# Transposing the SwiGLU activations on TensorE into PSUM instead of on VectorE in SBUF

## The reference

```
h = rms_norm(x); proj = h @ w_in                      # 1024 x 7428
merged = sum over 4 mixers of sigmoid(gate_n) * (mixer_n(proj) @ w_branch_n)
x = x + merged @ w_out                                # 1024 x 1024
h = rms_norm(x)
gate, up = split(h @ w_up)                            # 1024 x 2 * 2816
x = x + (silu(gate) * up) @ w_down                    # 2816 x 1024
```

## Time and profile before

| | before |
|---|---|
| median of 3 runs | 854.22 us |
| the profiled execution | 854.05 us |
| its span in the profile | 852.2 us |
| PE busy | 846.0 us (99%) |
| PE weight loads busy | 703.4 us (83%) |
| DVE busy | 665.1 us (78%) |
| ACT busy | 445.9 us (52%) |
| POOL busy | 114.8 us (13%) |
| DVE transposes (L1349), 192 instructions | 79.4 us |

### The profile page before, as it was taken

The page is one execution under the profiler, slowest core; times in us unless marked ns, Lnnn a source line. Parts: engine busy times, 40 slices in busy tenths (PEclk is TensorE's granted clock), DMA queues, the critical chain, the costliest instruction groups (busy, mean ns, idle before and its releaser), DMA issues.

```text
span 852.2 us, 11120 instructions
## 1 busy us (share of the span) xinstructions
PE 846.0 (99%) x4158; PEld 703.4 (83%) x4158; DVE 665.1 (78%) x1034; ACT 445.9 (52%) x646; POOL 114.8 (13%) x89
## 2 busy tenths in 40 slices
PE   9999999999999999999999999999999999999998
PEld 8888888888888888878888888888888888888787
DVE  7885967768778999985479668768697799999843
ACT  6557654754454444444365675558443644444441
POOL 0750201005502000000005402010054000000000
PEclk9999999999999999999999999999999999999999
DMA  9846655465567666556566365665655576666541
GB/s 341 289 156 188 201 181 173 145 227 194 177 196 241 197 195 192 191 187 192 154 188 185 112 194 163 198 198 146 221 186 169 168 225 196 198 197 194 178 148 49
DMA packets 87814, 160.46 MB, mean 188 GB/s; under 512 B 7504, under 2 KB 14160, under 8 KB 87760
## 3 DMA queue, kind: packets, MB, share of 16 engines
q1 hardware_dynamic: 87328, 159.09, 59.5%
q10 hardware_dynamic: 432, 0.66, 0.2%
HBM read 158.68 MB, written 1.05 MB: 187 GB/s over the span
## 4 chain that ended last, share of the span: by engine, by line
PE 96%; DVE 3%; issue 0%
PE bulk L1696 29%; PE bulk L1700 29%; PE bulk L1697 29%; PE bankAB L1444 2%; DVE wide L1349 2%; DVE w_lo L1024 1%; PE bulk L1752 1%; PE bankT L1601 0%; PE bankAB L1590 0%; PE bulk L1724 0%; PE bulk L1730 0%; PE bulk L1743 0%; PE bankAB L1548 0%; PE bankAB L1453 0%; DVE wide L1337 0%
## 5 line engine op out<-in xcount | busy, mean ns | idle before, releaser
L1024 DVE TENSOR_TENSOR w_lo<-raw,w_hi 128x1024 fp32r<-128x1024 f32 (+1 forms) x288 | 361.8, 1272 | 100.4 <-ACT w_hi L750 98.2
L750 ACT ACTIVATE w_hi<-raw 128x1024 fp32r<-128x1024 f32 (+1 forms) x286 | 296.6, 1047 | 244.9 <-PE bulk L1700 241.7
L1696 PE MATMUL bulk<-w_hi,hT_hi 128*128 128x512 f32 (+1 forms) x880 | 342.9, 390 | 0.0
L1697 PE MATMUL bulk<-w_lo,hT_hi 128*128 128x512 f32 (+1 forms) x880 | 339.2, 385 | 0.0
L1700 PE MATMUL bulk<-w_hi,hT_lo 128*128 128x512 f32 (+1 forms) x880 | 336.3, 386 | 0.0
L1696 PEld LDWEIGHTS bulk<-w_hi,hT_hi 128*128 128x128 f32 x880 | 165.3, 188 | 33.2 <-issue 0.5
L1700 PEld LDWEIGHTS bulk<-w_hi,hT_lo 128*128 128x128 f32 x880 | 165.0, 188 | 33.2
L1697 PEld LDWEIGHTS bulk<-w_lo,hT_hi 128*128 128x128 f32 x880 | 165.3, 188 | 31.8
L1349 DVE STREAM_TRANSPOSE wide<-wide 32x256 f32<-32x256 f32 (+1 forms) x192 | 79.4, 414 | 3.1
L1696 PE MATMUL bulk<-w_hi,aT_hi 128*128 128x512 f32 x174 | 68.0, 391 | 2.6 <-DVE wide L1337 2.6
L1700 PE MATMUL bulk<-w_hi,aT_lo 128*128 128x512 f32 x174 | 67.7, 389 | 0.0
(11 more groups left out here) (248 smaller groups left out, 708.9 us busy)
## 6 DMA issues: line engine op xcount, KB each, us to landing
raw<-in_w_in_dram SPq DMA_DIRECT2D x110, 512.0 KB, 4.2
raw<-in_w_ffn_up_dram SPq DMA_DIRECT2D x80, 512.0 KB, 3.8
raw<-in_w_ffn_down_dram SPq DMA_DIRECT2D x44, 512.0 KB, 3.4
raw<-in_w_branch_dram SPq DMA_DIRECT2D x20, 512.0 KB, 4.2
raw<-in_w_out_dram SPq DMA_DIRECT2D x16, 512.0 KB, 3.3
bias<-in_b_gate_dram SPq DMA_DIRECT2D x16, 256.0 KB, 4.7
raw<-in_w_ffn_up_dram SPq DMA_DIRECT2D x16, 256.0 KB, 3.5
raw<-in_w_in_dram SPq DMA_DIRECT2D x10, 256.0 KB, 2.6
```

The costliest lines, as they stand in the source:

```text
L750: act.activation(w_hi[:, g % RING, :, 0:width], raw[:, g % RAW, :, 0:width], ACT.Copy).then_inc(hi_ready, 1)
L1024: vec.tensor_tensor(w_lo[:, g % RING, :, 0:width], raw[:, g % RAW, :, 0:width], w_hi[:, g % RING, :, 0:width].bitcast(F32), ALU.subtract). ...
L1696: pe.matmul(dst, hi, whi, start=(k == ks[0]), stop=False)
L1697: pe.matmul(dst, hi, wlo, start=False, stop=False)
```

## The change

`act_turn` and its event go away. PE gets a stage `tr_act` p: for each token tile it waits for `ff_ready`, takes a bank (A and B for even p, T and O for odd p), and transposes the four blocks of 128 columns (two in the last part) into it. It stands at PE's slot FIRST(`ffu` p) + 6, for the last part at LAST(`fflast`) + 3. `act_evac` waits for that stage, reads the PSUM bank instead of `wide`, and stands at the same slot (before: three slots later; for the last part at LAST + 9). `ff_up` waits from p = 2 on until PE has read the buffer it overwrites.

```diff
+for _p in range(NPAIR):
+    _PE += [(FIRST[("ffu", _p)] + 6, "tr_act", _p)]
+_PE += [(LAST["fflast"] + 3, "tr_act", NPAIR)]
...
-FF_DONE = [FIRST[("ffu", _p)] + 4 for _p in range(NPAIR)] + [LAST["fflast"] + 1]
-FF_TURN = [_u + 1 for _u in FF_DONE[:-1]] + [FF_DONE[-1] + 4]
...
-        ffn += [(FIRST[("ffu", p)], "ff_gate", p)]
-    ffn += [(FF_DONE[NPAIR], "ff_gate", NPAIR)]
-    for p, u in enumerate(FF_DONE):
-        ffn += [(u, "ff_up", p), (FF_TURN[p] + 4, "act_evac", p)]
-        ffn += [(FF_TURN[p] + a, "act_turn", p, a) for a in range(NQUAD)]
+        ffn += [(FIRST[("ffu", p)], "ff_gate", p), (FIRST[("ffu", p)] + 4, "ff_up", p), (FIRST[("ffu", p)] + 6, "act_evac", p)]
+    ffn += [(LAST["fflast"] + 1, "ff_gate", NPAIR), (LAST["fflast"] + 1, "ff_up", NPAIR),
+            (LAST["fflast"] + 3, "act_evac", NPAIR),
...
             def act_evac(layer, p):                       # ACT
-                act.wait_ge(act_turned, nth(act_turned, layer, p))
-                for t in range(TT):
-                    lhs_part(layer, ("act", p, t), act_columns(aT[0], p, t), turned_act(p)[:, t, :, :])
+                blocks = 4 if p < NPAIR else 2
+                for t in range(TT):
+                    act.wait_ge(stage_done, nth(stage_done, layer, ("tr_act", p, t)))
+                    lhs_part(layer, ("act", p, t), aT[0][:, 4 * p:4 * p + blocks, t * P:(t + 1) * P],
+                             bank[("AB", "TO")[p % 2][t]][:, 0:blocks * P].rearrange("p (k q) -> p k q", k=blocks))
...
                     vec.wait_ge(ff_gated, nth(ff_gated, layer, (p, t)))
+                    if p >= 2:
+                        vec.wait_ge(stage_done, nth(stage_done, layer, ("tr_act", p - 2, t)))
...
-            def act_turn(layer, p, a):
-                if a == 0:
-                    vec.wait_ge(ff_ready, nth(ff_ready, layer, (p, 1)))
-                blocks, at = FF_BLOCKS[p], 2560 + 1024 * (p % 2)
-                tokens = slice(a * QUAD, (a + 1) * QUAD)
-                source = wide[tokens, :, at:at + blocks * P].rearrange("p t (k b q) -> p t k b q", b=NQUAD, q=QUAD)
-                for b in range(NQUAD):
-                    last = vec.transpose(turned_act(p)[b * QUAD:(b + 1) * QUAD, :, :, tokens], source[:, :, :, b, :])
-                if a == NQUAD - 1:
-                    last.then_inc(act_turned, 1)
...
+            def tr_act(layer, p):                         # PE
+                blocks = 4 if p < NPAIR else 2
+                for t in range(TT):
+                    pe.wait_ge(ff_ready, nth(ff_ready, layer, (p, t)))
+                    name = ("AB", "TO")[p % 2][t]
+                    take(name, lhs_lo, layer, ("act", p, t))
+                    for k in range(blocks):
+                        ins = pe.transpose(bank[name][:, k * P:(k + 1) * P], ff_act(t, p, blocks * P)[:, k * P:(k + 1) * P], identity)
+                    ins.then_inc(stage_done, 1)
```

More of the change, by code:

```diff
@@ L181, in stage_parts @@
         return [((stage, args[0], t), ("AB", "TO")[args[0]][t]) for t in range(TT)]
+    if stage == "tr_act":
+        return [((stage, args[0], t), ("AB", "TO")[args[0] % 2][t]) for t in range(TT)]
     raise ValueError(stage)
@@ L188 @@
         STAGE_EVENTS += [e for e, _ in stage_parts(*_s)]
-QUAD = 32
-NQUAD = P // QUAD
-FF_BLOCKS = [4] * NPAIR + [2]
-FF_DONE = [FIRST[("ffu", _p)] + 4 for _p in range(NPAIR)] + [LAST["fflast"] + 1]
-FF_TURN = [_u + 1 for _u in FF_DONE[:-1]] + [FF_DONE[-1] + 4]
 EARLY = [name for g, size in GROUPS.items() for name, last in LAST.items() if g <= last < g + size]
@@ L243, in evacuations @@
     for p in range(NPAIR):
-        ffn += [(FIRST[("ffu", p)], "ff_gate", p)]
-    ffn += [(FF_DONE[NPAIR], "ff_gate", NPAIR)]
-    for p, u in enumerate(FF_DONE):
-        ffn += [(u, "ff_up", p), (FF_TURN[p] + 4, "act_evac", p)]
-        ffn += [(FF_TURN[p] + a, "act_turn", p, a) for a in range(NQUAD)]
-    ffn += [(U - 3, "residual", "down", 0, 0), (U - 3, "gain", "attn", 0, 0),
+        ffn += [(FIRST[("ffu", p)], "ff_gate", p), (FIRST[("ffu", p)] + 4, "ff_up", p), (FIRST[("ffu", p)] + 6, "act_evac", p)]
+    ffn += [(LAST["fflast"] + 1, "ff_gate", NPAIR), (LAST["fflast"] + 1, "ff_up", NPAIR),
+            (LAST["fflast"] + 3, "act_evac", NPAIR),
+            (U - 3, "residual", "down", 0, 0), (U - 3, "gain", "attn", 0, 0),
             (U - 3, "residual", "down", 0, 1), (U - 3, "gain", "attn", 0, 1),
@@ L442, in ff_tmp @@
             return wide[:, t, 2048 + 1024 * (p % 2):2048 + 1024 * (p % 2) + width]
[L444 to L450, removed]
         def ff_act(t, p, width):
@@ L537, in build @@
         ff_ready = signal("ff_ready", [(p, t) for p in range(NPAIR + 1) for t in range(TT)])
-        act_turned = signal("act_turned", range(NPAIR + 1))
         def wait_item(engine, layer, name, t):
@@ L966, in _ @@
                           diff_evac=diff_evac, gate=nothing, sigmoid=sigmoid, branch=nothing,
-                          merged_evac=merged_evac, ff_gate=ff_gate, ff_up=nothing, act_turn=nothing, act_evac=act_evac)
+                          merged_evac=merged_evac, ff_gate=ff_gate, ff_up=nothing, act_evac=act_evac)
             def first_hi(k):
@@ L1339, in ff_up @@
                                              op1=ALU.mult).then_inc(ff_ready, 1)
-            def act_turn(layer, p, a):
-                if a == 0:
-                    vec.wait_ge(ff_ready, nth(ff_ready, layer, (p, 1)))
-                blocks, at = FF_BLOCKS[p], 2560 + 1024 * (p % 2)
-                tokens = slice(a * QUAD, (a + 1) * QUAD)
-                source = wide[tokens, :, at:at + blocks * P].rearrange("p t (k b q) -> p t k b q", b=NQUAD, q=QUAD)
-                for b in range(NQUAD):
-                    last = vec.transpose(turned_act(p)[b * QUAD:(b + 1) * QUAD, :, :, tokens], source[:, :, :, b, :])
-                if a == NQUAD - 1:
-                    last.then_inc(act_turned, 1)
             def act_evac(layer, p):
+                blocks = 4 if p < NPAIR else 2
                 for t in range(TT):
-                    lhs_rest(layer, ("act", p, t), act_columns(aT[1], p, t), turned_act(p)[:, t, :, :], act_columns(aT[0], p, t))
+                    dst = slice(4 * p, 4 * p + blocks)
+                    lhs_rest(layer, ("act", p, t), aT[1][:, dst, t * P:(t + 1) * P],
+                             bank[("AB", "TO")[p % 2][t]][:, 0:blocks * P].rearrange("p (k q) -> p k q", k=blocks),
+                             aT[0][:, dst, t * P:(t + 1) * P])
             def nothing(*_):
@@ L1367, in _ @@
                           diff_evac=diff_evac, gate=gate, sigmoid=nothing, branch=branch,
-                          merged_evac=merged_evac, ff_gate=ff_gate, ff_up=ff_up, act_turn=act_turn, act_evac=act_evac)
+                          merged_evac=merged_evac, ff_gate=ff_gate, ff_up=ff_up, act_evac=act_evac)
             vec.memset(warm[:, :], 0.0).then_inc(warm_ready, 1)
@@ L1639, in tr_merged @@
                     ins.then_inc(stage_done, 1)
+            def tr_act(layer, p):
+                blocks = 4 if p < NPAIR else 2
+                for t in range(TT):
[5 more added lines that the diff above has]
+                    ins.then_inc(stage_done, 1)
             stages = dict(tr_norm=tr_norm, tr_qk=tr_qk, tr_fox=tr_fox, tr_forget=tr_forget, tr_ss=tr_ss, cum=cum, pool_a=pool_a, pool_b=pool_b,
                           sb_scores=sb_scores, sb_sums=sb_sums, sb_out=sb_out, scores=scores, tr_probs=tr_probs, pv=pv,
-                          tr_diff=tr_diff, tr_merged=tr_merged)
+                          tr_diff=tr_diff, tr_merged=tr_merged, tr_act=tr_act)
             def lhs_of(name, k, t):
```

## The result

The changed kernel takes 861.22 us, median of four runs (861.15 to 861.28), against 854.26 us (854.05 to 854.47) before on the same chip: 7.0 us slower, ratio 1.008 with a 95% interval of 1.0067 to 1.0092. The forecast was 860.9 (859.3 to 863.5). Over all 15 executions on record, the changed kernel takes 860.89 to 861.28 us, so a difference of 0.2 us from 861.22 says nothing.

A forecast was written before the change was run, and what follows sets the result against it. The prediction took PE's instruction stream as the bound. Transposes at +9.94 us and the removed stall at -3.15, all else 0, made +6.8 us: 860.9 us, 0.8% slower, range 859.3 to 863.5.

The forecast's parts named there:

- PE's stream is the bound: Whole kernel: PE busy 846.0 of 852.2 us, matmuls 226.7 ns apart; DVE's load does not reach PE's rate.
- the rival on the other side: Matmuls during DVE's transposes: DVE's traffic on `wide` holds them back; at 10 ns each the change brings 852.5; chance 0.04.
- 88 transposes, 9.94 us: New PE work, 44 per layer: groups of eight cost 0.90 us, groups of four 0.47, together 9.94 us.
- The record's 0.272 us: Rival at the new PE transposes: each costs its record length, 23.9 us in all, giving 874.9; chance 0.02.
- The stall, -3.15 us: First unit of down 1: PE's wait for `ff_up` of the last part goes, 1.58 us per layer, 3.15 in both.
- The cover: At down 1: PE would be free at 367.76 and wants to go at 368.14, so the wait is hidden by 0.38 us.
- The added waits: PE at `tr_act` waiting for `ff_ready`: 3.8 us of slack for pair 4, 2.9 for the last part, so 0.
- the moved evacuation: `act_evac` on ACT and DVE, earlier and from PSUM: some 7 us of cover before PE needs the unit, so 0.
- `ff_up`'s new wait: On DVE, `ff_up` waits for a transposition put at 10 slots back, so 0.
- The sum: Whole kernel: +9.94 for the transposes, -3.15 for the stall, +6.8 us.
- DVE's busy time: Sign in the changed kernel's profile: DVE busy near 586 us (665.1 - 79.4).

The follow-up runs named there:

- run 2: The changed kernel with each of the 88 new PE transposes done twice in a row into the same place: 870.63 us.
- run 3: The changed kernel with only the first 128 columns of each tile transposed, 24 transposes in place of 88, waits and evacuations kept: 854.19 us.
- run 4: The changed kernel with DVE's 192 transposes put back as idle work, pair 4's last four ahead of `ff_gate` and `ff_up` of the last part: 870.14 us.
- run 1: The kernel before, transposes left on DVE, with `ff_up` of the last part moved ahead of pair 4's four transposes in DVE's order: 850.98 us.
- run 6: The changed kernel with `tr_act` of pairs 0 to 4 two slots earlier on PE, at FIRST + 4: 873.84 us.
- run 5: The changed kernel with DVE's 192 transposes back as idle work, pair 4's last four behind `ff_gate` and `ff_up` of the last part: 863.15 us.
- run 7: The changed kernel with the 88 transposes taking only 64 of the 128 tokens (64 streamed columns, half the array's rows): 861.05 us.
- run 9: The changed kernel with the 88 transposes taking 64 of 128 features of each block and 64 of 128 tokens: 860.05 us.

## Why the prediction was right

- **PE's stream is the bound, and its pace does not depend on DVE.** The first is shown by runs 2 and 3 (every transposition is paid, at 0.107 and 0.110 us), the second by the equal counts of run 4 and the changed kernel. That also answers the rival on the other side, in which DVE's traffic slows the matmuls.
- **88 transposes, 9.94 us.** The ten groups came at 0.90 and the two at 0.47 us, the numbers read before from other places of the kernel. The record's 0.272 us, and the figure of the Trainium skill beside it ("TensorE: Matmul & The Clock Gate", section "Part 4: PE-mode transpose"), are lengths and not costs in this stream: 88 more of them cost 9.4 us in run 2 where the page's 275 ns would give an estimate of 24. Nor did they lower the clock: it was granted at 1.000 in the changed kernel and in run 2, with sixteen in a row.
- **The stall, -3.15 us, gone whole.** PE has no wait there. Run 1 gives the same amount by itself: 3.16 us in its trace, 3.3 by the medians. The cover was said to be 0.38 us and is about 0.6: `ff_up` starts at 371.58, PE would be free 0.63 us later, at 372.21, and goes at 372.80.
- **The added waits and the moved evacuation, 0.** Right as put: 3.8 us of slack at `ff_ready`; run 6 shows what it is worth. One distance was misread, without consequence: `ff_up`'s new wait is for a transposition 14 slots back, not 10.
- **What is left.** The sum was +6.79 us, the two spans differ by 7.00. Laid side by side matmul by matmul, the traces part into three terms. At 8.3 us, far ahead of the change, the changed kernel is already 0.09 us later; such a difference is in run 1's trace too (0.27 us), so it belongs to the start of the program and not to the change. The twelve groups cost 10.07 us where the sum has 9.94, since the slightly slow steps go on past the fifth matmul behind a group. The two stalls give back 3.16. DVE's busy time was put at 586 us and is 589.4. Its other instructions take as long as before, added up one by one, within 0.4 us; but records of neighbours overlap, by 37.8 us before and 34.3 now, and the page counts overlapping time once.
- **Where my reading was too easy.** I wrote that the stall was one place of DVE lateness and took its disappearance as a gain of the change, though I had DVE's order at that slot in front of me. It was only the order of two stages, which run 1 swaps without the change; a lateness at that place can cost more than the wait itself, as run 4 shows.

## What to carry to other kernels

Moving work from an engine that is busy but early to the one whose stream sets the end costs its whole start-to-start price, less only what that stream had waited for the old work, however much time the other engine gets free. Read that price from the starts around the same operation at another place of the kernel, not from the length of its record. And when a wait would go away with a large change, first try to reorder the two stages that make it: here that alone gave 3.3 us, and the large change lost 7.0.

## What the runs showed of the hardware

- A wait of PE of 1.3 us before, 0.75 in run 5 and 0.8 in run 6 left the granted clock at 1.00. After the wait of 2.68 us in run 4 (2.71 in layer 1) the clock was at its lower level, 1.2 GHz (0.50), for about eight matmul starts, and with that each lateness of 2.84 us cost some 4.45.
- A float32 transposition on PE starts 0.11 us after the one before with 128 streamed columns, whether 128 or 64 columns are loaded, and on average 0.07 us (run 7) or 0.06 us (run 9) with 64 streamed columns on 64 rows.
- Between matmuls on all 128 rows, a group on 64 rows loses the overlap of its weight load at both ends: the first load starts 0.32 us behind the last full matmul instead of with it, and the next full matmul 0.15 us behind the last transposition instead of 0.03.
